# Scores of the differential heads: three fp32r products of split operands in place of one fp32 product, with a new tile order

## The chip, the cores and the metric

One core of a Trainium2 chip runs the whole kernel in one launch. The metric is the device time in microseconds of that launch, the median of several runs.

## What is computed

The kernel is one decoder layer over 512 positions of width 1024, in fp32. The normalised input `n` is projected by one wide matrix to the inputs of three branches: A, causal differential attention (8 heads, two softmax maps of 64 channels each per head, with a relative-position bias); B, a gated DeltaNet (8 heads, in chunks); C, cross-attention (4 heads) into 256 memory tokens. Each branch is projected, the three are merged by sigmoid gates, projected again and added to the input; a squared-ReLU MLP follows. The change touches branch A:

```python
s = jnp.einsum('bqhmd,bkhmd->bhmqk', qi, k, preferred_element_type=jnp.float32) * scale
s = s + bias;  s = jnp.where(dist >= 0, s, -jnp.inf)
p = jax.nn.softmax(s, axis=-1)
w = p[:, :, 0] - lam * p[:, :, 1]
o = jnp.einsum('bhqk,bkhe->bqhe', w.astype(v.dtype), v)
```

with 8 heads `h`, two maps `m`, 64 channels `d`, and 128 value channels `e`.

## The kernel before

**Main tiles.** All large products run on TensorE (PE) by weight tiles of 1024 x 128. A weight tile is loaded by DMA into `w_raw`, rounded by ScalarE (ACT, L1107) to the fp32r buffer `w_hi`, and VectorE (DVE, L1404) writes the rest to `w_lo`. In `weight_tile` PE then makes three fp32r products for each of 8 blocks of rows: high by high (L1903), low input by high weight (L1904), high input by low weight (L1905), each with 512 moving columns (256 for the 16 tiles of the memory, whose input is `m_hi`, `m_lo`). A tile's sum lies in one of two PSUM banks, `acc[:, t % 2]`; ACT copies it out ("evac", L1171 for the cross queries `cq`, L1175 for `aq`, `ak`, `av` of a head), and PE waits for that copy before it starts tile t + 2 (`acc_free`).

**Steps between the main tiles.** In the mixing part (up to about 790 us) the tiles are cut in quarters, and between the quarters PE makes the steps of the branches. Attention has, for every head h, the steps `av` (transposes of v, L2007), `as0` and `as1` (scores, L2012), `at` (transposes of the weights, L2018), `ap` (weights by v, L2023) and `ay` (transposes of the output, L2027); before them cross-attention has `cs` (scores, L1991), `ct` (L1997) and `cv` (L2002) for each of 4 heads. Each step waits for ACT and DVE to finish the step before it: DVE adds the bias (L1560) and takes the maxima (L1566), ACT takes the exponentials (L1231), DVE normalises and subtracts (L1584, L1588), and so on. The delta steps of branch B (L2046 to L2103, with many 32 x 32 products in L2062, L2066, L2068) run the same way for four pairs of heads.

**Scores.** `as0` makes the three largest score blocks that fit three PSUM banks, `as1` the other five. A block of map m and query block q has its 64 channels in rows 64m to 64m + 63 of PE's array, 128 queries as stationary columns and (q + 1) x 128 keys as moving columns. The operands lie in `qkv_T`, fp32, buffered for two heads:

```python
score_parts = {"as0": ((0, 3, 0), (1, 3, 512), (0, 1, 1280)),
               "as1": ((1, 2, 640), (0, 2, 128), (1, 1, 1280), (0, 0, 0), (1, 0, 512))}
```

(map, query block, first PSUM column).

**The order of the work.** `ORDER` (L89) gives the order of the main tiles by hand. `mixing_tiles` expands it and says in `need_free` which step must be over before a tile may be copied out: the tiles of heads 0 and 1 wait for the last `cv` (their place in SBUF held the cross-attention's data), those of head h for `as1` or `av` of head h - 2. `plan_order` then simulates the engines with the costs in `PE_US`, `ACT_US`, `DVE_US` and others, and gives each engine a fixed order of its work; PE takes a delta step before an attention step before a main quarter when each is ready by the plan. The plan is made when the kernel is built; on the chip every engine runs its own order and waits on semaphores.

**Memory.** The softmax weights lie in `p_a` (two maps), their transposes in `wT`, a buffer of its own. `hold` keeps 1280 columns free; after it `mv_T`, `cq_T` and `qkv_T` share one place at different times.

Of the kernel before, what the change touches and what calls it, by code (L numbers as in the profile page):

```python
# [29 lines left out]
P = 128  # L30
# [44 lines left out]
         "sb": 1.35, "cs": 3.44, "cv": 3.43, "as0": 1.3, "as1": 1.35, "at": 1.09, "ap": 2.24, "av": 0.44, "ay": 0.44}  # L75
# [132 lines left out]
def plan_order(tiles, need_free, n_first):  # L208
# [30 lines left out]
    old = lambda n: n >= n_first - 1  # L239

    for t in range(n_first, n_mix):
        for n, (a, b) in enumerate(parts[t]):
            add("PE", "main", ("main", t, a, b), (b - a) * (0.36 if short(t) else 0.681),
                [("DVE", "lo", t), ("ACT", "evac", t - 2)] if n == 0 else [])
# [72 lines left out]
    for i, (kind, h) in enumerate(attn):  # L317
# [26 lines left out]
    for r in range(2):  # L344
# [3 lines left out]
            "DVE": ("lo", "delta", "attn", "conv", "fin", "finz", "pre"), "POOL": ("delta", "gate", "pre"),  # L348
# [89 lines left out]
def build(nc, weights, x, mem, w_ba, params, consts, onehot, relb, post_g, y_dram, gate_dram, f_dram, frep_dram, out):  # L438
# [13 lines left out]
    n_z = {t: i for i, t in enumerate(z_tiles)}  # L452
    n_gate = {t: i for i, t in enumerate(gate_tiles)}
# [3 lines left out]
    with ExitStack() as ctx:  # L457
# [71 lines left out]
        def part_of(buf, n, width=QB):  # L529
# [38 lines left out]
        c3 = ExitStack()  # L568
        s3 = sb_in(c3)
        qkv_T = s3("qkv_T", [P, 2, 3, S])  # L570
        onehot_sb = strip[0:BUCKETS, 0:2, :].rearrange("p a b -> p (a b)")[:, 0:SPAN]
        c3.close()
# [87 lines left out]
        lam_exp = sem("lam_exp")  # L660
        a_mm = sem("a_mm")
# [58 lines left out]
        f_row = qkv_T[0:HA, 1, 2, 0:SPAN]  # L720
# [18 lines left out]
                       "as1": ((1, 2, 640), (0, 2, 128), (1, 1, 1280), (0, 0, 0), (1, 0, 512))}  # L739
        score_cols = {"as0": slice(0, 3), "as1": slice(3, 8)}  # L740
# [359 lines left out]
        def _(act):  # L1100
# [54 lines left out]
            def evacuate(t):  # L1155
# [16 lines left out]
                elif kind in ("aq", "ak", "av"):  # L1172
                    if (kind, j) == ("av", 1):
                        act.wait_ge(f_out, 16)
                    last = nc.scalar.copy(qkv_T[:, j % 2, ("aq", "ak", "av").index(kind)], bank)  # L1175
# [201 lines left out]
        def _(dve):  # L1377
# [192 lines left out]

            def attn_scale(i):
# [104 lines left out]
            def reload_hi(kk):  # L1676

                dve.wait_ge(y_pre[kk % 2], 16 * (kk // 2 + 1))
                if kk == 0:
# [5 lines left out]
                        "mem_norm": memory_norm, "mem_gain": memory_gain, "mem_lo": memory_lo}  # L1685
# [155 lines left out]
        def _(pe):  # L1841
# [99 lines left out]
            def main_part(t, k0, k1):  # L1941
# [32 lines left out]
            def attn(i):  # L1974
# [29 lines left out]
                elif kind == "av":  # L2004
                    pe.wait_ge(acc_free, TILES.index(("av", h)) + 1)
                    for s in range(ST):
                        last = nc.tensor.transpose(ps_a[:, 0, s * P:(s + 1) * P], qkv_T[:, h % 2, 2, s * P:(s + 1) * P], ident)  # L2007
# [379 lines left out]
```

## Time and profile before

| | us |
|---|---|
| median of 3 runs (lowest, highest) | 1335.35 (1334.2, 1338.17) |
| profiled execution, its own time | 1335.78 |
| its span from first to last instruction | 1334.0 |
| PE busy in the span | 1310.9 |
| DVE busy | 763.4 |
| ACT busy | 461.9 |

The profile shows one execution of the kernel. A matmul's time in it runs from its start to the end of its passage through the array, so that matmuls overlap; what one costs PE is the distance from its start to the start of the next. PE's weight loads have a line of their own (PEld). An fp32 product stands as two records, an fp32r product as one.

### The profile page before, as it was taken

The page shows a single profiled execution, that of the slowest core. Times are in us where ns is not written, and L with a number is a line of the kernel's source. Part 1 is how long each engine was busy: PE and PEld are TensorE (multiplying, and loading weights), DVE is VectorE, ACT ScalarE, POOL GpSimd, SP SyncE. Part 2 cuts the span into 40 slices and gives each one's busy share as a digit, 9 for nine tenths or more (in the row PEclk, how much of TensorE's full clock was granted, in tenths as well). Part 3 has the DMA queues.
Part 4 walks back from the last instruction along what each step waited for, and adds up shares of the span by engine and source line. Part 5 has one row for each costly group of instructions (what it writes and reads, how often), then busy time and mean ns, then how long its engine had stood idle before and what let it go on. Part 6 is the DMA issues. An engine that isn't in the chain of part 4 may idle for free.

```text
span 1334.0 us, 23822 instructions
## 1 busy us (share of the span) xinstructions
PE 1310.9 (98%) x10193; PEld 1094.6 (82%) x10193; DVE 763.4 (57%) x1305; ACT 461.9 (35%) x765; POOL 186.5 (14%) x128
## 2 busy tenths in 40 slices
PE   9999999999999999999999999999989999999997
PEld 8789988787788887888878888888788788888786
DVE  6885335576676577568955354555675522355335
ACT  5443433343353443443434222112432212222220
POOL 1023000013000023000321412233012200022000
PEclk9999999999999999999999999999999999999999
DMA  6155413222212322212222636644422333233311
GB/s 217 66 177 166 125 48 111 79 95 64 75 56 79 102 97 85 63 62 97 71 89 97 185 123 218 210 157 149 174 65 94 95 111 101 89 98 101 101 63 63
DMA packets 62832, 144.03 MB, mean 108 GB/s; under 512 B 5072, under 2 KB 28168, under 8 KB 62728
## 3 DMA queue, kind: packets, MB, share of 16 engines
q1 hardware_dynamic: 62728, 142.51, 33.1%
q8 instruction: 81, 1.33, 0.4%
q14 instruction: 23, 0.19, 0.0%
HBM read 127.79 MB, written 16.27 MB: 108 GB/s over the span
## 4 chain that ended last, share of the span: by engine, by line
PE 88%; DVE 7%; issue 3%; ACT 2%; DMA 1%; POOL 0%; SPq 0%; DVEq 0%; ACTq 0%; POOLq 0%
PE acc L1903 17%; PE acc L1905 16%; PE acc L1904 16%; PE ps_a L1904 2%; PE ps_a L1903 2%; PE ps_a L1905 2%; PE ps_a L2012 2%; PE ps_d L2090 2%; PE ps_a L2219 2%; PE ps_d L2219 2%; PE ps_a L2220 2%; PE ps_d L2220 2%; PE ps_d L2221 2%; PE ps_a L2221 2%; DVE w_lo L1404 1%
## 5 line engine op out<-in xcount | busy, mean ns | idle before, releaser
L1404 DVE TENSOR_TENSOR w_lo<-w_raw,w_hi 128x1024 fp32r<-128x1024 f32 x170 | 233.4, 1373 | 205.6 <-ACT w_hi L1107 205.0
L1107 ACT CAST w_hi<-w_raw 128x1024 fp32r<-128x1024 f32 x170 | 178.0, 1048 | 407.0 <-PE acc L1905 331.8
L1903 PE MATMUL acc<-n_hi,w_hi 128*128 128x512 f32 x744 | 303.2, 408 | 0.0
L1905 PE MATMUL acc<-n_hi,w_lo 128*128 128x512 f32 x744 | 290.7, 391 | 0.0
L1904 PE MATMUL acc<-n_lo,w_hi 128*128 128x512 f32 x744 | 290.2, 390 | 0.0
L1905 PEld LDWEIGHTS acc<-n_hi,w_lo 128*128 128x128 f32 x744 | 139.6, 188 | 30.2
L1903 PEld LDWEIGHTS acc<-n_hi,w_hi 128*128 128x128 f32 x744 | 139.9, 188 | 29.2 <-issue 2.2
L1904 PEld LDWEIGHTS acc<-n_lo,w_hi 128*128 128x128 f32 x744 | 140.1, 188 | 25.9 <-issue 0.7
L1095 POOL TENSOR_TENSOR h_lo<-sq,h_hi 128x512 fp32r<-128x512 f32 x32 | 41.4, 1293 | 276.4 <-DVE h_hi L1819 276.4
L1903 PE MATMUL acc<-y_hi,w_hi 128*128 128x512 f32 x192 | 74.8, 390 | 0.0
L1905 PE MATMUL acc<-y_hi,w_lo 128*128 128x512 f32 x192 | 74.7, 389 | 0.0
L1904 PE MATMUL acc<-y_lo,w_hi 128*128 128x512 f32 x192 | 74.7, 389 | 0.0
L1404 DVE TENSOR_TENSOR wx_lo<-w_raw,wx_hi 128x1024 fp32r<-128x1024 f32 x27 | 42.7, 1582 | 55.5 <-ACT wx_hi L1107 55.5
L1078 POOL TENSOR_SCALAR gate_st<-gate_st 128x512 f32<-128x512 f32 x24 | 25.3, 1056 | 310.0 <-ACT gate_st L1189 310.0
L1342 ACT ACTIVATE sq<-relu 128x512 f32<-128x512 f32 x32 | 20.2, 632 | 118.7 <-DVE relu L1817 118.7
L1520 DVE SCALAR_TENSOR_TENSOR conv_y<-conv_x,par,conv_y 128x512 f32<-128x512 f32 x72 | 57.2, 794 | 2.6
L1107 ACT CAST wx_hi<-w_raw 128x1024 fp32r<-128x1024 f32 x27 | 28.2, 1043 | 52.0 <-PE acc L2221 28.7
L1049 POOL TENSOR_TENSOR sums_hi<-cst,par 128x1024 fp32r<-128x1024 f32 x4 | 8.4, 2103 | 262.6 <-PE ps_d L2046 150.2
L1903 PEld LDWEIGHTS acc<-y_hi,w_hi 128*128 128x128 f32 x192 | 36.0, 188 | 7.7
L1905 PEld LDWEIGHTS acc<-y_hi,w_lo 128*128 128x128 f32 x192 | 36.0, 188 | 7.5
L1904 PEld LDWEIGHTS acc<-y_lo,w_hi 128*128 128x128 f32 x192 | 36.0, 188 | 7.3
L1231 ACT ACTIVATE p_a<-ps_a,smd 128x512 f32<-128x512 f32 (+3 forms) x64 | 32.9, 529 | 16.7 <-DVE smd L1568 16.7
(424 smaller groups left out, 2465.7 us busy)
## 6 DMA issues: line engine op xcount, KB each, us to landing
w_raw<-weights SPq DMA_DIRECT2D x200, 512.0 KB, 3.5
gate_scratch<-gate_st SPq DMA_DIRECT2D x24, 256.0 KB, 4.2
g_in<-gate_scratch SPq DMA_DIRECT2D x24, 256.0 KB, 3.9
y_raw<-y_scratch SPq DMA_DIRECT2D x16, 256.0 KB, 3.7
x_tok<-x SPq DMA_DIRECT2D x4, 512.0 KB, 5.2
y_scratch<-y_st SPq DMA_DIRECT2D x4, 512.0 KB, 2.7
y_scratch<-d_ET SPq DMA_DIRECT2D x4, 512.0 KB, 2.7
y_scratch<-y_st SPq DMA_DIRECT2D x8, 256.0 KB, 2.3
```

The lines of the kernel that those rows point to most:

```text
L1095: nc.gpsimd.tensor_tensor(h_lo[:, f % 16], sq[:, f % 2], h_hi[:, f % 16].bitcast(F32), ALU.subtract).then_inc(hl_ok, 1)
L1107: nc.scalar.copy(hi_of_tile(t), w_raw[:, t % RAW]).then_inc(hi_ready, 1)
L1231: last = nc.scalar.activation(p_a[:, m, pack_of[q]:pack_of[q] + w], flat(ps_a[:])[:, col:col + w], ACT.Exp, bias=nbs[:, n:n + 1], scale=SC ...
L1404: V_.tensor_tensor(lo_of_tile(t), w_raw[:, t % RAW], hi_of_tile(t).bitcast(F32), ALU.subtract).then_inc(lo_ready, 1)
L1520: ins = V_.scalar_tensor_tensor(out=y, in0=conv_x[:, n % 2, j:j + S], scalar=par[:, col + j:col + j + 1], in1=y, op0=ALU.mult, op1=ALU.add)
L1903: mm(bank, wh, hi_of(k), start=start and k == 0, stop=False)
L1904: mm(bank, wh, lo_of(k), start=False, stop=False)
L1905: last = mm(bank, wl, hi_of(k), start=False, stop=stop and k == KT - 1)
L2012: last = mm(ps[:, col:col + (q + 1) * P], qkv_T[rows_m, h % 2, 0, q * P:(q + 1) * P], qkv_T[rows_m, h % 2, 1, 0:(q + 1) * P], start=True, ...
L2219: mm(to, high, wh, start=kb == 0, stop=False)
L2220: mm(to, low, wh, start=False, stop=False)
L2221: return mm(to, high, wl, start=False, stop=kb == 2 * KT - 1)
```

## The change

1. `aq` and `ak` are copied out by ACT into an fp32r buffer `qk_hi`, and DVE writes the rest, `acc - qk_hi`, to `qk_lo` (a new step `scores_lo`, two for each head). `av` goes to `v_T`.
2. Each score block is the sum of three fp32r products: high by high, high queries by low keys, low queries by high keys. Blocks are taken in groups, and a block of one query block (128 keys) is made 256 columns wide, the rest being overwritten later.
3. PE waits in `as0` for the low part of the head's keys, and before main tile t + 2 for the low part of tile t if that is `aq` or `ak`. The planner has the same two waits, and a cost of 0.75 us for the DVE step.
4. `wT` is now `p_a[:, 1]`, `hold` is gone, and the places of the buffers of queries and keys change.
5. `ORDER` and the planner's costs of `as0` and `as1` change.

```diff
-"as0": 1.3, "as1": 1.35
+"as0": 1.05, "as1": 1.2
...
-ORDER = [("first", 0), ("z", 0), ("mem", 0), ("cq", 0), ("cq", 1), ("cq", 2), ("cq", 3), ("conv", 1), ("head", 0),
-         ("head", 1), ("gate", 1), ("conv", 2), ("head", 2), ("gate", 2), ("head", 3), ("z", 1), ("gate", 1),
-         ("head", 4), ("gate", 2), ("z", 2), ("head", 5), ("conv", 3), ("head", 6), ("gate", 2), ("head", 7),
-         ("gate", 13), ("z", 3)]
+ORDER = [("first", 0), ("z", 0), ("mem", 0), ("gate", 1), ("cq", 0), ("cq", 1), ("cq", 2), ("conv", 1), ("cq", 3),
+         ("head", 0), ("conv", 2), ("head", 1), ("head", 2), ("z", 1), ("gate", 1), ("head", 3), ("head", 4),
+         ("z", 2), ("conv", 3), ("gate", 5), ("head", 5), ("gate", 2), ("head", 6), ("gate", 3), ("head", 7),
+         ("gate", 3), ("z", 3), ("gate", 6)]
...
+            if kind in ("aq", "ak"):
+                add("DVE", "qk", ("qk", t), 0.75, [("ACT", "evac", t)])
...
+        if kind == "as0":
+            deps.append(("DVE", "qk", of[("ak", h)]))
...
-        wT = sa_("wT", [P, 10 * P])
+        wT = p_a[:, 1]
...
-        hold = sa_("hold", [P, 1280])
...
+        qk_hi = s3("qk_hi", [P, 2, 2, S], F32R)
+        qk_lo = s3("qk_lo", [P, 2, 2, S], F32R)
+        v_T = s3("v_T", [P, 2, S])
...
+        product_groups = {"as0": (((0, 3, 0), (1, 3, 512)), ((0, 1, 1280),)),
+                          "as1": (((0, 0, 0), (1, 0, 512)), ((0, 2, 128), (1, 2, 640)), ((1, 1, 1280),))}
...
+                dve.wait_ge(acc_free, t + 1)
+                V_.tensor_tensor(qk_lo[:, place[0], place[1]], acc[:, t % 2], qk_hi[:, place[0], place[1]].bitcast(F32),
+                                 ALU.subtract).then_inc(qkl_ready, 1)
...
+                    if TILES[t - 2][0] in ("aq", "ak"):
+                        pe.wait_ge(qkl_ready, qk_tiles.index(t - 2) + 1)
...
-                    for m, q, col in score_parts[kind]:
-                        rows_m = slice(DA * m, DA * m + DA)
-                        last = mm(ps[:, col:col + (q + 1) * P], qkv_T[rows_m, h % 2, 0, q * P:(q + 1) * P],
-                                  qkv_T[rows_m, h % 2, 1, 0:(q + 1) * P], start=True, stop=True)
+                    if kind == "as0":
+                        pe.wait_ge(qkl_ready, 2 * h + 2)
+                    for group in product_groups[kind]:
+                        for n, (left, right) in enumerate(((qk_hi, qk_hi), (qk_hi, qk_lo), (qk_lo, qk_hi))):
+                            for m, q, col in group:
+                                rows_m = slice(DA * m, DA * m + DA)
+                                width = max(q + 1, 2) * P
+                                last = mm(ps[:, col:col + width], left[rows_m, h % 2, 0, q * P:(q + 1) * P],
+                                          right[rows_m, h % 2, 1, 0:width], start=n == 0, stop=n == 2)
```

In `ORDER`, "first" stands for 9 tiles (6 of the convolution, 3 gates), "mem" for 16 tiles of 256 columns, "conv" for 6, "head" for 3 (`aq`, `ak`, `av`), "cq" and "z" for 2, and ("gate", n) for n tiles.

## Rows read from the trace of the kernel before

**Rows 1.** The page, part 1: busy time of each engine.

```profile
PE 1310.9 (98%) x10193; PEld 1094.6 (82%) x10193; DVE 763.4 (57%) x1305; ACT 461.9 (35%) x765; POOL 186.5 (14%) x128
```

**Rows 2.** Busy time by stretch: length, then PE, PEld, DVE, ACT, POOL.

```profile
0.00:133.40 133.40, 129.05 (x1242) 114.85 (x1243) 97.24 (x176) 60.48 (x92) 24.55 (x19) 1.00 0.47 157
133.40:300.00 166.60, 166.60 (x1339) 138.82 (x1337) 81.25 (x129) 65.36 (x114) 5.66 (x3) 1.00 0.28 92
300.00:360.00 60.00, 59.05 (x1081) 47.27 (x1080) 37.88 (x72) 22.48 (x46) 11.63 (x6) 1.00 0.24 73
360.00:500.00 140.00, 140.00 (x842) 116.12 (x841) 97.26 (x201) 61.88 (x122) 8.72 (x6) 1.00 0.26 82
500.00:667.00 167.00, 165.66 (x1825) 136.45 (x1825) 125.80 (x238) 70.57 (x139) 28.17 (x16) 1.00 0.24 75
667.00:770.00 103.00, 101.19 (x1353) 83.75 (x1351) 49.61 (x101) 36.24 (x66) 25.46 (x21) 1.00 0.42 127
```

**Rows 3.** Waits of the whole kernel: who, for whom, total, times, longest.

```profile
ACT w_hi L1107 <- PE acc L1905: 331.8, 105, 6.7
...
PE ps_a L2027 <- DVE o_a L1596: 1.3, 1, 1.3
PE ps_d L2066 <- DVE d_XB L1639: 1.1, 2, 0.7
```

**Rows 4.** PE groups by form: busy, mean ns of one; score products and a full-array fp32 form.

```profile
L2002 PE MATMUL ps_a<-pT_c,mv_tok 128*128 128x512 f32 x32 | 14.4, 592 | 0.0
...
L2012 PE MATMUL ps_a<-qkv_T 64*128 64x512 f32 x32 | 9.0, 641 | 0.0
```

**Rows 5.** Timeline around the first score step of a head.

```profile
516.44 0.39 PE L1905 MATMUL acc<-n_hi,w_lo 128*128 128x512 f32 x1
...
516.67 0.40 PE L1903 MATMUL acc<-n_hi,w_hi 128*128 128x512 f32 x1
...
516.91 0.39 PE L1904 MATMUL acc<-n_lo,w_hi 128*128 128x512 f32 x1
...
517.14 0.40 PE L1905 MATMUL acc<-n_hi,w_lo 128*128 128x512 f32 x1
...
517.46 1.55 PE L2012 MATMUL ps_a<-qkv_T 64*128 64x512 f32 x6
...
518.95 0.26 PE L2066 MATMUL ps_d<-d_TT,d_XB 32*32 32x32 f32 x8
```

**Rows 6.** The same step, weight loads only.

```profile
517.46 0.30 PEld L2012 LDWEIGHTS ps_a<-qkv_T 64*128 64x128 f32 x4 [0.36 <-issue]
518.00 0.19 PEld L2012 LDWEIGHTS ps_a<-qkv_T 64*128 64x128 f32 x1 [0.23 <-issue]
518.43 0.19 PEld L2012 LDWEIGHTS ps_a<-qkv_T 64*128 64x128 f32 x1 [0.24 <-issue]
```

**Rows 7.** Timeline around the second score step of the same head.

```profile
529.32 1.56 PE L2012 MATMUL ps_a<-qkv_T 64*128 64x384 f32 x10
530.81 0.50 PE L1903 MATMUL acc<-n_hi,w_hi 128*128 128x512 f32 x1
531.15 0.40 PE L1904 MATMUL acc<-n_lo,w_hi 128*128 128x512 f32 x1
531.39 0.40 PE L1905 MATMUL acc<-n_hi,w_lo 128*128 128x512 f32 x1
```

**Rows 8.** Timeline in the memory tiles, whose products have 256 columns.

```profile
96.53 0.28 PE L1904 MATMUL acc<-m_lo,w_hi 128*128 128x256 f32 x1
...
96.64 0.28 PE L1905 MATMUL acc<-m_hi,w_lo 128*128 128x256 f32 x1
...
96.76 0.28 PE L1903 MATMUL acc<-m_hi,w_hi 128*128 128x256 f32 x1
```

**Rows 9.** Chain of waits: start, us. The cross-attention of one head, with fp32 products.

```profile
226.14 3.45 PE ps_a L1991 x16
...
237.77 0.87 PE ps_a L1997 x8
...
241.38 3.43 PE ps_a L2002 x8
...
247.54 3.45 PE ps_a L1991 x16
...
259.18 0.87 PE ps_a L1997 x8
...
262.82 3.43 PE ps_a L2002 x8
```

**Rows 10.** DVE groups by form: the nearest to the added subtraction.

```profile
L1404 DVE TENSOR_TENSOR w_lo<-w_raw,w_hi 128x1024 fp32r<-128x1024 f32 x170 | 233.4, 1373 | 205.6 <-ACT w_hi L1107 205.0
...
L1771 DVE TENSOR_TENSOR g_tmp<-acc,g_in 128x512 f32<-128x512 f32 x16 | 11.1, 692 | 39.2 <-PE acc L1905 39.2
```

**Rows 11.** ACT group: copies of head tiles out of the accumulator.

```profile
L1175 ACT COPY qkv_T<-acc 128x512 f32<-128x512 f32 x24 | 14.0, 582 | 0.0
```

More of the change, by code:

```diff
@@ L74 @@
 PE_US = {"dE": 0.91, "dL": 1.79, "dA": 1.79, "dU": 1.79, "dW": 1.79, "T1": 0.55, "Za": 0.55, "Wb": 1.05, "Z5": 0.55, "W5": 0.9, "Zl": 1.2, "Wl": 1.2, "sa": 0.45,
-         "sb": 1.35, "cs": 3.44, "cv": 3.43, "as0": 1.3, "as1": 1.35, "at": 1.09, "ap": 2.24, "av": 0.44, "ay": 0.44}
+         "sb": 1.35, "cs": 3.44, "cv": 3.43, "as0": 1.05, "as1": 1.2, "at": 1.09, "ap": 2.24, "av": 0.44, "ay": 0.44}
 ACT_US = {"dk": 2.1, "dL": 1.6, "Wb": 0.45, "Z5": 0.45, "W5": 2.1, "Zl": 0.62, "sb": 0.45, "cs": 2.9, "as0": 2.3, "as1": 2.9, "at": 1.5, "ap": 0.65,
@@ L239, in plan_order @@
     old = lambda n: n >= n_first - 1
+    split_of = lambda t: [("DVE", "qk", t)] if tiles[t][0] in ("aq", "ak") else []
     for t in range(n_first, n_mix):
@@ L243, in plan_order @@
             add("PE", "main", ("main", t, a, b), (b - a) * (0.36 if short(t) else 0.681),
-                [("DVE", "lo", t), ("ACT", "evac", t - 2)] if n == 0 else [])
+                [("DVE", "lo", t), ("ACT", "evac", t - 2)] + split_of(t - 2) if n == 0 else [])
     for t in range(n_first + SPL - 1, n_mix + SPL):
@@ L347, in plan_order @@
     rank = {"PE": ("delta", "attn", "main"), "ACT": ("hi", "evac", "delta", "attn", "fin", "finz"),
-            "DVE": ("lo", "delta", "attn", "conv", "fin", "finz", "pre"), "POOL": ("delta", "gate", "pre"),
+            "DVE": ("lo", "qk", "delta", "attn", "conv", "fin", "finz", "pre"), "POOL": ("delta", "gate", "pre"),
             "SP": ("load", "gate", "y", "yb", "bias", "pre")}
@@ L452, in build @@
     n_z = {t: i for i, t in enumerate(z_tiles)}
+    qk_tiles = [t for t in range(N_MIX) if TILES[t][0] in ("aq", "ak")]
     n_gate = {t: i for i, t in enumerate(gate_tiles)}
@@ L553, in build @@
         p_a = sa_("p_a", [P, 2, 10 * P])
-        wT = sa_("wT", [P, 10 * P])
+        wT = p_a[:, 1]
         v_tok = sa_("v_tok", [P, S])
         o_a = sa_("o_a", [P, ST, P])
-        hold = sa_("hold", [P, 1280])
+        c3 = ExitStack()
+        s3 = sb_in(c3)
+        s3("before_qk", [P, 512])
+        qk_hi = s3("qk_hi", [P, 2, 2, S], F32R)
+        qk_lo = s3("qk_lo", [P, 2, 2, S], F32R)
+        v_T = s3("v_T", [P, 2, S])
+        c3.close()
+        sa_("before_cq", [P, 2560])
         c3 = ExitStack()
@@ L567, in build @@
         c3.close()
-        c3 = ExitStack()
-        s3 = sb_in(c3)
-        qkv_T = s3("qkv_T", [P, 2, 3, S])
         onehot_sb = strip[0:BUCKETS, 0:2, :].rearrange("p a b -> p (a b)")[:, 0:SPAN]
-        c3.close()
         c2.close()
@@ L660, in build @@
         lam_exp = sem("lam_exp")
+        qkl_ready = sem("qkl_ready")
         a_mm = sem("a_mm")
@@ L719, in build @@
         ealog = sml[:, 64:64 + HB]
-        f_row = qkv_T[0:HA, 1, 2, 0:SPAN]
+        f_row = v_T[0:HA, 1, 0:SPAN]
         p_a_scr = flat(conv_qk[:, 0, 0])
@@ L1171, in evacuate @@
                     last = nc.scalar.copy(cq_T[:, (j // 2) % 2, j % 2], bank)
-                elif kind in ("aq", "ak", "av"):
-                    if (kind, j) == ("av", 1):
+                elif kind in ("aq", "ak"):
+                    last = nc.scalar.copy(qk_hi[:, j % 2, ("aq", "ak").index(kind)], bank)
+                elif kind == "av":
+                    if j == 1:
                         act.wait_ge(f_out, 16)
-                    last = nc.scalar.copy(qkv_T[:, j % 2, ("aq", "ak", "av").index(kind)], bank)
+                    last = nc.scalar.copy(v_T[:, j % 2], bank)
                 elif kind in ("dq", "dk", "dv"):
@@ L1569, in attn, with scores_lo @@
                                      ALU.mult).then_inc(a_max, 1)
+            def scores_lo(t):
+                kind, h = TILES[t]
+                place = (h % 2, ("aq", "ak").index(kind))
+                dve.wait_ge(acc_free, t + 1)
+                V_.tensor_tensor(qk_lo[:, place[0], place[1]], acc[:, t % 2], qk_hi[:, place[0], place[1]].bitcast(F32),
+                                 ALU.subtract).then_inc(qkl_ready, 1)
             def attn_scale(i):
@@ L1684, in _ @@
                         "pre": reload_hi, "beta_in": beta_and_decay_inputs, "beta": beta_and_decay,
-                        "mem_norm": memory_norm, "mem_gain": memory_gain, "mem_lo": memory_lo}
+                        "qk": scores_lo, "mem_norm": memory_norm, "mem_gain": memory_gain, "mem_lo": memory_lo}
             for kind, *n in ORDER_OF["DVE"]:
@@ L2006, in attn @@
                     for s in range(ST):
-                        last = nc.tensor.transpose(ps_a[:, 0, s * P:(s + 1) * P], qkv_T[:, h % 2, 2, s * P:(s + 1) * P], ident)
+                        last = nc.tensor.transpose(ps_a[:, 0, s * P:(s + 1) * P], v_T[:, h % 2, s * P:(s + 1) * P], ident)
                 elif kind in ("as0", "as1"):
                     ps = flat(ps_a[:])
-                    for m, q, col in score_parts[kind]:
-                        rows_m = slice(DA * m, DA * m + DA)
-                        last = mm(ps[:, col:col + (q + 1) * P], qkv_T[rows_m, h % 2, 0, q * P:(q + 1) * P],
-                                  qkv_T[rows_m, h % 2, 1, 0:(q + 1) * P], start=True, stop=True)
+                    if kind == "as0":
[7 more added lines that the diff above has]
+                                          right[rows_m, h % 2, 1, 0:width], start=n == 0, stop=n == 2)
                 elif kind == "at":
```

## The prediction

> **What bounds the kernel now.** I read the page's busy shares first, then the busy time by stretch, then PE's own waits, then the places of the change. PE is busy for 1310.9 of 1334.0 us [rows 1]. Busy time of pipelined matmuls proves little alone, so the stretches matter: in the mixing part after 133.4 us PE has no idle time up to 300, and 0.95, 0, 1.34 and 1.81 us in the four stretches from 300 to 770 us, 4.1 us in all [rows 2]. The longest wait there is 1.3 us, in `ay`, for DVE [rows 3]. ACT in turn waits for PE for 331.8 us before it rounds the next weights [rows 3], so the supply of weights is behind PE's pace and not ahead of it. DVE is at 97.3 of 140 and 125.8 of 167 us in the dense stretches [rows 2]: high, with some room. So here the time is the sum of what PE issues. What PE saves is saved, if the fixed order of the work does not turn it into waiting.
>
> **Part 1, the score products.** A main product of 512 columns starts 0.23 us after the one before it [rows 5], one of 256 columns 0.11 to 0.12 us after [rows 8]; both are fp32r. An fp32 product is two records, each 0.43 us for 512 columns (8 in 3.43 us) and 0.215 us for 256 (16 in 3.45 us) [rows 9]. So one fp32 product costs 0.86 us where three fp32r ones cost 0.69: the change wins 0.17 us at 512 columns and about 0.07 at 256 (0.43 against 0.36), and loses at 128, which it makes 256 wide.
>
> The score blocks of the two maps lie in different halves of the array, and as fp32 they run two at a time: the 32 records of 512 columns last 641 ns each, 20.5 us one after the other, and cover 9.0 us [rows 4]; four weight loads pass in 0.30 us [rows 6]. Step `as0` should then cost 2 x 0.43 for the pair and 2 x 0.215 for the single block, 1.29 us. It takes 518.95 - 517.46 = 1.49 [rows 5]. The other 0.20 is at its ends: a first weight load that nothing hides, and the change to other work. I keep it. `as1` takes 530.81 - 529.32 = 1.49 as well [rows 7].
>
> After the change, if fp32r pairs run together too: `as0` is 3 x 0.23 (pair of 512) + 3 x 0.12 (single 256) + 0.20 = 1.25 us. `as1` is 3 x 0.12 (pair of 256) + 3 x 0.175 (pair of 384, midway between the two rows) + 3 x 0.12 + 0.20 = 1.44. The saving is 0.24 + 0.05 = 0.29 us a head, **2.3 us** for 8 heads, of 23.8 us that the sixteen steps take. Bounds of it: if weight loads of a pair come one after the other, nothing is left of it (pairs that don't overlap at all are a rival below); if the 0.20 at the ends goes too, 2.3 + 3.2 = 5.5 us.
>
> The trace has no fp32r pair on half the rows, so this term hangs on the pairing. The Trainium skill (TensorE: Matmul & The Clock Gate, Part 3, The mechanism) says that a weight load overlaps a matmul in flight only when the row group differs. By that rule each of the 15 steps of a head would bear a bare load. The main stream speaks against it: its loads all go to the same rows and its products are still 0.23 us apart [rows 5].
>
> **Part 2, DVE's subtraction.** 16 instructions of 128 x 512 from PSUM. The nearest rows are 0.69 us with a PSUM operand, and 1.37 us for twice the columns written as fp32r [rows 10]; I take 0.69, 11 us of DVE in 470 us. It lies beside PE. ACT's copies keep their number and their 0.58 us [rows 11].
>
> **Part 3, the new waits.** PE waits before tile t + 2 for the subtraction of tile t. Behind that wait stands everything on PE. The bank used to be free about 0.6 us after the tile's last product, and is now free after 0.6 + 0.7 + hops, some 1.5 us; PE needs it one tile later, 8 x 3 x 0.23 = 5.5 us. Cover: 4 us. It fails only if DVE comes more than 4 us late to the subtraction; what could hold it are items of up to 4.5 us by the plan, so a wait now and then of 1 us is possible, and I put 0 to 2 us for all 16, and 0.3 in the sum. The wait in `as0` is for `ak`, which is followed by the whole tile `av` and its transposes: nothing. On DVE the subtraction waits for ACT's copy, with the weight splits, on which PE's next tile hangs, queued behind it. These have run up to three tiles ahead: nothing.
>
> **Part 4, buffers.** `wT` in `p_a[:, 1]`: the second map is dead once the difference is formed, before `at` is copied out, and the squares that DVE puts there follow `ap`. The steps of attention are already serial. Nothing, and no bound but a planner's shift.
>
> **Part 5, the order.** The same tiles, 24 gates among them; the work of PE is equal. What can change is idle time and how many times PE changes between main tiles and steps. One change costs 0.32 - 0.23 = 0.09 us going in [rows 5] and 0.34 - 0.23 = 0.11 coming back [rows 7], 0.2 together. There are 62 attention and 116 delta steps; 10 more or fewer that stand alone are 2 us. The 4.1 us of idle time [rows 2] are the most that a better order can take away beside that. The new order lays five gates behind the last convolution and spreads seven of the thirteen that stood at the end; this should thin out DVE where it is dense. I take 1.3 us as gained (a third of the idle time), with ends of 6 gained and 6 lost.
>
> **Sum** against the profiled execution: 1335.8 - 2.3 + 0.3 - 1.3 = 1332.5. That execution lies 0.4 above the median, so I predict **1332.1 us**. Differences under 0.3%, 4 us, are about what a measurement of this kernel cannot tell from none; the forecast is inside it.
>
> **Rivals.**
> *The order gives more.* PE's idle time goes (4.1 us) and ten to fifteen lone steps join others (2 to 3 us): 1335.4 - 2.3 - 6.5 = 1326.6. For it: the idle time sits at single steps that came too early by under 1.5 us [rows 3], as a plan with wrong costs gives. Against it: the plan's costs of the other steps stay as they were. Chance of passing 4 us in all: 0.35.
>
> *The pairs run one after the other.* At fp32r each half of the array would deliver a column in half the time of an fp32 record. If PSUM or the array cannot take both streams, `as0` gets 3 x 0.23 and `as1` 3 x (0.12 + 0.175) more, 1.57 us a head, 12.6 in all: 1335.4 - 3.3 + 12.6 = 1344.7, slower. It decides from 18% of lost overlap (2.3 of 12.6) for the saving to be gone, and from 58% (7.3 of 12.6) for a slower kernel. Against it: the fp32 pairs show no loss, their step of 0.43 being that of the full array [rows 9], and the moving rows read are 64 + 64, as many as a main product reads. The fp32 records last somewhat longer in pairs (641 against 592 ns [rows 4]). Chance 0.07. The same page of the Trainium skill (Part 3, Measured speedup vs the span model) gives 3.07 for four row tiles; an estimate from it, with 77% of the ideal, is 30% on the pairs, 3.8 us, and a time of 1335.9. A loss of that size I give 0.07, counted as no change.
>
> *The cross-attention blocks head 0.* `cq` 3 now stands right before head 0, whose copies wait for the last `cv`. A cross head takes 18.7 us from `cs` to the end of `cv` [rows 9], so head 0's `av` tile can start about 0.6 + 0.5 + 18.7 + 1.7 = 21.5 us after `cq` 3. PE has two main tiles (11.0) and the three steps themselves (7.75), 18.8; one or two delta steps of 1.8 us close the gap. If DVE, with six convolution tiles just behind it, makes the chain 10 us longer, PE stands for that time: 1335.4 - 2.0 + 8 = 1341. It decides from some 5 us of delay. Against it: cross heads have run 21.4 us apart [rows 9], and pair 1 of the delta work becomes ready there. Chance 0.08.
>
> *Something else takes the saving* (the subtraction late in dense stretches, more lone steps), and the time stays within 2 us of before: inside "no change", with my forecast.
>
> **How the numbers follow.** Forecast and its neighbours within 4 us: 0.43, partial overlap 0.07, so "same" 0.50. Better order: 0.35. Serial pairs and the blocked head: 0.15. The range of 1325.5 to 1341.0 takes in the better order with its ends and the blocked head, and leaves out the serial pairs.
>
> **What would show it.** Right: `as0` 1.25 us and `as1` 1.44 us from first product to the next work, 24 records a head; pairs of 512 columns 0.23 us apart; sixteen subtractions near 0.69 us; PE idle in 300 to 770 us not over 4 us; no wait of PE for `qk_lo` over 1 us. Wrong: `as0` near 1.9 us (serial pairs); a wait of PE of several us before the first `av` tile; PE's idle time in the mixing part changed by more than the scores save.

## The result and the profile after

The changed kernel takes 1338.56 us (12 runs, 1335.94 to 1340.49), the kernel before 1335.27 (12 runs, 1333.22 to 1338.17): a ratio of 1.0023, 95% interval 1.0015 to 1.0031. It is slower by 3.3 us, clear of noise, though inside the 0.3% that the prediction called no change. I had forecast 3.2 us faster. The profiled execution took 1337.14 us, 1.4 below the median of its kernel and 1.4 above the profiled one of before; what the profiles show is the smaller part of the difference. One sign of being right failed, by little: PE is idle for 4.2 us in 300 to 770 us, where I had set 4.

The scores first. The timeline of `as0` of one head in the changed kernel, with the columns of [rows 5]:

```profile
550.57 0.50 PE L2041 MATMUL ps_a<-qk_hi 64*128 64x512 f32 x2
550.91 0.40 PE L2041 MATMUL ps_a<-qk_lo,qk_hi 64*128 64x512 f32 x2
551.14 0.39 PE L2041 MATMUL ps_a<-qk_hi,qk_lo 64*128 64x512 f32 x2
551.37 0.28 PE L2041 MATMUL ps_a<-qk_hi 64*128 64x256 f32 x1
551.49 0.28 PE L2041 MATMUL ps_a<-qk_lo,qk_hi 64*128 64x256 f32 x1
551.61 0.27 PE L2041 MATMUL ps_a<-qk_hi,qk_lo 64*128 64x256 f32 x1
551.81 0.50 PE L1925 MATMUL acc<-n_hi,w_hi 128*128 128x512 f32 x1
```

The pairs run together, 0.23 us from one pair to the next; the step takes 551.81 - 550.57 = 1.24 us where it took 1.49 [rows 5]. The 16 steps, `as0` and `as1`, take 21.4 us by the distances between starts, against 23.8. This part of the change does what was said.

Then the busy time by stretch of the changed kernel (length, then PE, PEld, DVE, ACT, POOL, as in [rows 2]), and below it three of PE's waits, as in [rows 3]:

```profile
133.40:300.00 166.60, 165.55 (x1590) 139.05 (x1588) 92.00 (x138) 65.78 (x116) 18.14 (x9) 1.00 0.27 87
300.00:360.00 60.00, 60.00 (x967) 47.89 (x954) 37.64 (x63) 25.72 (x52) 0.00 (x0) 1.00 0.23 72
360.00:500.00 140.00, 138.93 (x1223) 116.14 (x1221) 96.52 (x201) 54.74 (x102) 19.23 (x9) 1.00 0.25 80
500.00:667.00 167.00, 163.91 (x1734) 137.23 (x1720) 120.56 (x237) 70.44 (x137) 23.02 (x16) 1.00 0.26 83
667.00:770.00 103.00, 103.00 (x1037) 87.13 (x1025) 59.03 (x134) 41.49 (x84) 6.74 (x8) 1.00 0.30 93
770.00:933.80 163.80, 162.01 (x718) 133.34 (x717) 79.93 (x104) 35.98 (x37) 52.91 (x36) 1.00 0.59 186
```

```profile
PE ps_a L2047 <- DVE p_a L1610: 3.0, 1, 3.0
...
PE acc L1925 <- POOL y_lo L1084: 1.8, 2, 1.0
...
PE ps_a L2056 <- DVE o_a L1618: 0.9, 1, 0.9
```

From 133 to 934 us PE is idle for 1.05 + 0 + 1.07 + 3.09 + 0 + 1.79 = 7.0 us; before it was 4.1, all of it ahead of 770. The small old gaps are mostly gone. In their place `at` of head 5 (counted from 0) waits 3.0 us in one piece for VectorE (DVE), where the longest wait was 1.3 us, and the first products of the branches wait twice for `y_lo`, 1.8 us in all, which GpSimd (POOL) writes. So of the profiled 1.4 us, 2.9 are added idle time and -2.4 the scores; the other 0.9 is spread over the start (0.3) and changes too small to place.

**Why DVE was late.** The timeline of DVE and, in the second fence, of POOL in the changed kernel, around that wait:

```profile
635.17 7.41 DVE L1606 TENSOR_SCALAR p_a<-p_a,smd 128x128 f32<-128x128 f32 x4
642.62 1.94 DVE L1610 SCALAR_TENSOR_TENSOR p_a<-p_a,smd 128x128 f32<-128x128 f32 x4
```

```profile
635.10 2.38 POOL L1069 TENSOR_TENSOR d_SCR<-d_XB,cst 128x1024 f32<-128x1024 f32 x1 [3.10 <-ACT d_XB L1274]
637.41 0.96 POOL L1072 MEMSET d_TF<- 128x1024 f32 x1
638.32 2.00 POOL L1074 TENSOR_TENSOR d_KB<-d_K,e_in 128x1024 f32<-128x1024 f32 x1
640.40 1.90 POOL L1076 TENSOR_TENSOR d_K<-d_K,k_fac 128x1024 f32<-128x1024 f32 x1
```

Four multiplications by a scalar for each row, which take 1.27 us together where POOL is quiet, took 7.41 us, until POOL's fourth instruction was over. In the kernel before, no head's multiplications were lengthened so (the longest of the 32 took 0.48 us). Weight splits were, which take 1.22 us in the median; one of them in that kernel, begun beside an instruction of POOL of 2.48 us:

```profile
514.10 3.40 DVE L1404 TENSOR_TENSOR w_lo<-w_raw,w_hi 128x1024 fp32r<-128x1024 f32 x1
```

PE did not wait for it. What is new in the changed kernel is not that the two engines hold one another up, but which instruction of DVE it hits.

**Why `y_lo` was late.** The last `ay` came at 754.6 us in place of 731.8. The data of the first branch are read back only then, since their place in SBUF is attention's; the last `y_lo` was ready at 794.3, with the first branch tile due at 787.4. Before, it was ready at 768.0, 20 us ahead of its tile. How far attention moved can be counted in `ORDER`: ahead of head 7 stood 8 gate tiles (beside the three of "first"), now 12, and all other tiles there are the same. A tile is 24 products, 5.5 us, so four tiles are 22 us, and the last `ay` came 22.8 us later.

### The profile page after: what moved, and what is told of

Same layout as the page of the kernel before. It is cut to its first block, busy times and chain, and to the rows that moved or that the text cites. A ratio compares the mean times of both kernels' runs of the same rounds, so it can differ in the third digit from the quotient of the medians.

```text
span 1335.4 us, 23967 instructions
## 1 busy us (share of the span) xinstructions
PE 1309.1 (98%) x10257; PEld 1097.8 (82%) x10257; DVE 771.6 (58%) x1321; ACT 462.4 (35%) x765; POOL 186.1 (14%) x128
## 4 chain that ended last, share of the span: by engine, by line
PE 88%; DVE 6%; issue 2%; DMA 2%; ACT 1%; POOL 1%; SPq 0%; DVEq 0%; ACTq 0%; POOLq 0%
PE acc L1925 16%; PE acc L1927 16%; PE acc L1926 16%; PE ps_a L1926 2%; PE ps_a L1925 2%; PE ps_a L1927 2%; PE ps_d L2119 2%; PE ps_d L2248 2%; PE ps_a L2248 2%; PE ps_d L2249 2%; PE ps_a L2250 2%; PE ps_a L2249 2%; PE ps_d L2250 2%; PE ps_a L2041 2%; PE ps_a L2052 1%
## 5 line engine op out<-in xcount | busy, mean ns | idle before, releaser
L1418 DVE TENSOR_TENSOR w_lo<-w_raw,w_hi 128x1024 fp32r<-128x1024 f32 x170 | 229.7, 1352 | 173.1 <-ACT w_hi L1119 172.0
L1090 POOL TENSOR_SCALAR gate_st<-gate_st 128x512 f32<-128x512 f32 x24 | 22.4, 931 | 477.3 <-ACT gate_st L1203 477.3
L1925 PE MATMUL acc<-m_hi,w_hi 128*128 128x256 f32 x128 | 37.5, 293 | 0.0
L1927 PE MATMUL acc<-m_hi,w_lo 128*128 128x256 f32 x128 | 36.1, 282 | 0.7 <-issue 0.7
```

The lines of the kernel that those rows point to most:

```text
L1418: V_.tensor_tensor(lo_of_tile(t), w_raw[:, t % RAW], hi_of_tile(t).bitcast(F32), ALU.subtract).then_inc(lo_ready, 1)
L1925: mm(bank, wh, hi_of(k), start=start and k == 0, stop=False)
L1927: last = mm(bank, wl, hi_of(k), start=False, stop=stop and k == KT - 1)
```

## The experiments

Theory A: the order costs (collision and late end), the scores save 2.3 us. Rival B: the split operands cost, by the subtraction and the longer hold of the bank. Rival C: the scatter between executions. "The kernel before" in each ratio was run on the same chip in the same session.

### The order alone

```diff
-ORDER = (that of before)
+ORDER = (that of after)
```

in the kernel before, nothing else.

> The kernel before with the new ORDER and nothing else: fp32 scores, no subtraction, old buffers. Theory A (the order is what costs, the scores save 2.3 us as their steps do in the trace): 3.3 + 2.3, so about 5.5 us above the kernel before (1341), with the long wait of PE for head 5's normalisation and the waits for y_lo ahead of the first branch tile again there. Rival B (the split operands cost: the subtraction, the bank held longer, the waits on it): the order alone is within 1.5 us of the kernel before. Rival C (the scatter between runs is the cost, whatever the order): within 2 us, with runs spread over 4 us.

1349.54 us (4 runs), ratio 1.0113 (1.0100 to 1.0126). Every theory was far off. PE's waits in its profile:

```profile
PE acc L1903 <- POOL y_lo L1072: 7.2, 5, 2.9
PE ps_d L2068 <- issue: 3.3, 2, 1.9
```

The new order without the planner's new costs and waits gives another plan: attention ends at 777.6 us, the last `y_lo` is ready at 806.1, and PE waits 7.2 us. That is not the whole of it:

```profile
791.00:800.00 9.00, 4.94 (x12) 2.52 (x12) 4.11 (x5) 0.83 (x2) 5.33 (x5) 0.81 0.45 139
800.00:812.00 12.00, 8.82 (x21) 5.94 (x21) 3.11 (x5) 1.05 (x1) 4.69 (x4) 0.57 0.75 232
```

The granted clock (third column from the right) fell behind the waits to a mean of 0.81 and 0.57, that is to the lower of its two levels (1.2 in place of 2.4 GHz) for a good part of 21 us. The clock is at 0.50 for 13.6 of them, which costs 6.8 us. The predicted collision of head 5 is not in this profile.

### The scores alone

```diff
-ORDER = (that of after)
+ORDER = (that of before)
```

in the changed kernel.

> The changed kernel with the old ORDER (split operands, three fp32r products, shared buffer, costs of the planner as changed). Theory A: 2.3 us under the kernel before, about 1333.0, PE idle in the mixing part about as in the kernel before. Rival B: at or above the kernel before (1335 to 1339). If both the order and the scores are innocent alone and cost together (the plan depends on both), neither this nor the order alone is slower.

1345.5 us (6 runs, 1341.71 to 1351.24), ratio 1.0087 (1.0067 to 1.0107). Theory A falls in the form in which I had it: the parts don't add. Each half costs 11 to 15 us and both together 3.3. The wait that I had put at 0.3 us is here, in PE's waits:

```profile
PE acc L1925 <- DVE qk_lo L1590: 6.4, 3, 2.3
```

The timeline of one of the three, PE, ACT and DVE:

```profile
327.86 1.25 PE L2047 MATMUL ps_a<-cst,p_a 128*128 128x128 f32 x10
...
328.11 1.05 ACT L1119 CAST w_hi<-w_raw 128x1024 fp32r<-128x1024 f32 x1 [3.61 <-PE acc L1927]
...
329.19 1.23 DVE L1418 TENSOR_TENSOR w_lo<-w_raw,w_hi 128x1024 fp32r<-128x1024 f32 x1 [1.19 <-ACT w_hi L1119]
...
330.33 0.68 DVE L1590 TENSOR_TENSOR qk_lo<-acc,qk_hi 128x512 fp32r<-128x512 f32 x1
...
331.16 0.47 PE L1925 MATMUL acc<-n_hi,w_hi 128*128 128x512 f32 x1 [2.05 <-DVE qk_lo L1590]
```

The subtraction stands in DVE's fixed order behind a weight split. The split waits for ACT's rounding, and that for the last product of PE's own tile, whose weights it overwrites (idle 3.61 us until PE). So the subtraction cannot come before PE has ended its tile, and PE's next tile waits for the subtraction: rounding, split and subtraction, 1.05 + 1.23 + 0.68, pass with PE idle but for one step. The profiled execution was the fastest of the six; the profile does not show what the slower ones, up to 1351 us, had beside these waits.

### GpSimd held back in the changed kernel

```diff
                 elif kind == "dL":
                     pool.wait_ge(d_act, dA[i + 1])
+                    if p == 3:
+                        pool.wait_ge(a_dve, aD[a_idx[("as1", 5)] + 1])
```

> The changed kernel, with GpSimd waiting in step dL of pair 3 until head 5's normalisation is over, so that the two don't run side by side. In the trace of the changed kernel the four multiplications of that head took 8.5 us instead of 1.5 beside four GpSimd instructions, and PE then waited 3.0 us. Theory A1 (they contend for a port): the four take about 1.5 us, PE's wait of 3 us goes, and the time falls by 2 to 3 us to about 1336. Rival (VectorE was slow there for another reason, or PE would wait for GpSimd instead): the multiplications stay long, or the time does not move by more than 1 us.

1335.9 us (11 runs), ratio 1.0005 (0.9996 to 1.0014): 0.0018 of the time, 2.4 us, under the changed kernel's ratio. DVE's row there:

```profile
635.41 1.27 DVE L1608 TENSOR_SCALAR p_a<-p_a,smd 128x128 f32<-128x128 f32 x4
```

The four take 1.27 us and PE's wait is gone. Theory A1 holds: beside GpSimd the multiplications are held up, and that costs about what PE waited (2.4 us in the times, 3.0 in the profile; the two intervals only just don't touch). GpSimd's work now falls beside a weight split of DVE. First DVE, then POOL:

```profile
639.09 3.24 DVE L1420 TENSOR_TENSOR w_lo<-w_raw,w_hi 128x1024 fp32r<-128x1024 f32 x1 [0.42 <-ACT w_hi L1121]
642.25 0.68 DVE L1592 TENSOR_TENSOR qk_lo<-acc,qk_hi 128x512 fp32r<-128x512 f32 x1
```

```profile
638.84 2.40 POOL L1071 TENSOR_TENSOR d_SCR<-d_XB,cst 128x1024 f32<-128x1024 f32 x1 [6.61 <-DVE p_a L1612]
642.10 1.99 POOL L1076 TENSOR_TENSOR d_KB<-d_K,e_in 128x1024 f32<-128x1024 f32 x1
```

The split takes 3.24 us, and PE does not wait for it. The subtraction, which reads one operand from PSUM, keeps its 0.68 us beside GpSimd.

### Products of one map after those of the other

```diff
-                        for n, (left, right) in enumerate(((qk_hi, qk_hi), (qk_hi, qk_lo), (qk_lo, qk_hi))):
-                            for m, q, col in group:
+                        for m, q, col in group:
+                            for n, (left, right) in enumerate(((qk_hi, qk_hi), (qk_hi, qk_lo), (qk_lo, qk_hi))):
```

> The changed kernel with the three products of one block issued one after the other and then those of the other map's block, so that neighbours use the same half of the array. If the pairing is worth what the prediction says: as0 gains 3 x 0.23, as1 3 x (0.12 + 0.175), 1.57 us a head, some 12.6 us in all, 1351; a little less because the last product of one map and the first of the other still overlap. If fp32r products of the two halves never really ran together, the time does not change.

1338.95 us (8 runs), ratio 1.0028 (1.0018 to 1.0038), as the changed kernel. By my expectation that would mean that pairs never ran together. The timeline says otherwise:

```profile
321.69 0.51 PE L2041 MATMUL ps_a<-qk_hi 64*128 64x512 f32 x2
322.03 0.40 PE L2041 MATMUL ps_a<-qk_lo,qk_hi 64*128 64x512 f32 x2
322.26 0.40 PE L2041 MATMUL ps_a<-qk_hi,qk_lo 64*128 64x512 f32 x2
```

The program now has three products of map 0 and then three of map 1, and they still start two by two. So they start out of the order of the program: the reading is that PE takes a product for the free half of the array ahead of older ones that wait for the other half. That nothing between the program and PE changed the order is not shown; the two of a pair start 10 ns apart here and 3 to 4 ns apart in the changed kernel. The experiment could not undo the pairing and says nothing on its worth.

### The old order with the subtraction ahead of the split

```diff
+    act, dve = order["ACT"], order["DVE"]
+    for item in [i for i in dve if i[0] == "qk"]:
+        k = dve.index(item)
+        while dve[k - 1][0] == "lo" and act.index(("evac", item[1])) < act.index(("hi", dve[k - 1][1])):
+            dve[k - 1], dve[k], k = dve[k], dve[k - 1], k - 1
```

in `plan_order`, with `ORDER` of before.

> The changed scores with the old ORDER, and the subtraction moved ahead of the weight split that stands just before it on VectorE wherever ScalarE copies the tile out before it rounds those weights. In the trace with the old ORDER, PE waited three times 2.2 us for the subtraction, which stood behind a split that itself waited for PE's own tile. Theory B1 (that place in VectorE's order is what costs): the three waits (6.4 us) go, and with them the fall of the clock at 614 us or some of it; the time is 1333 to 1337. Rival (VectorE is simply too full for 16 more instructions): PE waits elsewhere for as long, and the time stays at 1342 or above.

1342.66 us (6 runs, 1337.1 to 1343.8), ratio 1.0047 (1.0032 to 1.0062). The waits for `qk_lo` are gone from its profile, and with them 0.4% of the time; B1 holds for that part. But 0.47% remains, and the time lies in the rival's range and not in B1's. In this profile, of the fastest of the six, PE's idle time from 133 to 934 us is 4.9 us against 4.1 before, so in it the waits did not come back elsewhere, which the rival needs. PE waits in it at 606 to 609 us for DVE at two delta and attention steps:

```profile
606.77 0.63 PE L2061 MATMUL ps_a<-cst,o_a 128*128 128x128 f32 x4 [0.96 <-DVE o_a L1623]
608.94 1.20 PE L2127 MATMUL ps_d<-state,d_SCR 128*128 128x128 f32 x4 [1.54 <-DVE d_LT L1691]
...
611.20 0.63 PE L1932 MATMUL acc<-n_hi,w_lo 128*128 128x512 f32 x1
611.62 0.63 PE L1930 MATMUL acc<-n_hi,w_hi 128*128 128x512 f32 x1
```

Behind them main products start 0.42 us apart in place of 0.23: the clock is at its lower level, for 6.8 us. What held the slower executions up no profile here shows.

### Head 5 three gates earlier

```diff
-         ("z", 2), ("conv", 3), ("gate", 5), ("head", 5), ("gate", 2), ("head", 6), ("gate", 3), ("head", 7),
+         ("z", 2), ("conv", 3), ("gate", 2), ("head", 5), ("gate", 5), ("head", 6), ("gate", 3), ("head", 7),
```

> The changed kernel with head 5 after two gate tiles instead of five (the other three behind it). In the changed kernel attention ended 23 us later than before (754 against 732 us), the high and low parts of the first branch's data came until 794 us, and PE waited 2 us for them. Theory A2 (the late end of attention is what PE pays for there): attention ends some 10 us earlier, and the wait for y_lo is gone. The plan around heads 5 to 7 changes too, so the collision of head 5 with GpSimd may be gone or another may come: the whole time is between 1333 (both gone) and 1339. Rival (GpSimd or the loads are too slow there whenever attention ends): the wait for y_lo stays.

1338.88 us (10 runs), ratio 1.0025 (1.0016 to 1.0034). A miss: attention ended at 764.5 us, later and not earlier. The collision was gone, other waits came (1.7 us for `o_a`, 1.8 us in a step of small products, 1.1 us for `qk_lo`, `y_lo` again), and the time was the same. The count of tiles says why theory A2 had no chance here: head 5 stands three gates earlier, but the three stand behind it, and ahead of head 7, which ends attention, are 12 gates as in the changed kernel. What made it 10 us later still, the profile does not single out.

### Both mends

GpSimd held back, and the subtraction ahead of the split, in the changed kernel with its own order.

> The changed kernel with GpSimd's wait of the earlier run and the subtraction ahead of the weight splits. With the new ORDER PE never waited for the subtraction, so if theory B1 is right for the old ORDER only, this is equal to the run with GpSimd's wait alone (1335.9) within 1.5 us. If the subtraction costs in the new ORDER through VectorE's lateness, it is faster by 1 to 3 us.

1334.72 us (11 runs), ratio 0.9994 (0.9986 to 1.0003), against 1.0005 for the first mend alone. The second is worth 0.0011, 1.5 us, with intervals that overlap, although the profile of the changed kernel shows no wait for `qk_lo`. That it lies in DVE's lateness elsewhere is not shown.

### The read-back sooner

```diff
+    for k in range(1, len(order["SP"])):
+        if order["SP"][k][0] == "pre" and order["SP"][k - 1][0] == "gate":
+            order["SP"][k - 1], order["SP"][k] = order["SP"][k], order["SP"][k - 1]
...
+                dve.wait_ge(yh_ready, kk + 1)
+                V_.tensor_tensor(y_lo[0][:, kk], y_st[:, kk % 2], y_hi[0][:, kk].bitcast(F32),
+                                 ALU.subtract).then_inc(yl_ready, 1)
...
-            pool_work = {"gate": scale_gate, "delta": delta, "pre": lambda kk: y_lo_tile(0, kk)}
+            pool_work = {"gate": scale_gate, "delta": delta, "pre": lambda kk: None}
```

on top of both mends.

> The run with both mends, and the first branch's data read back sooner: its low part is made on VectorE right behind the high part instead of on GpSimd, where it stood behind gates that wait for PE's own tiles, and SyncE issues each read-back ahead of the gate store just before it. Theory A2 (the late reload is what PE pays for ahead of the first branch tile): PE's wait for y_lo (1.2 us in the profile of the run with both mends) is gone, and with it at times a fall of the clock: 1332 to 1334 in the median, under the kernel before by 0.1 to 0.3%. Rival (the loads themselves come too late because attention ends at 751 us): the wait stays and the time too, 1334.7.

1333.93 us (12 runs, 1330.2 to 1336.35), ratio 0.9985 (0.9975 to 0.9995). PE no longer waits for `y_lo`, although attention ended at 754.7 us, as late as in the changed kernel: the way of the data back was what PE waited for, not the end of attention alone. Against the run with both mends (0.9994) the gain lies inside the intervals. The profile has one new gap near 329 us, with the clock lower behind it (0.62, third column from the right). PE's wait there, and the busy time of the stretch behind it:

```profile
PE ps_d L2110 <- issue: 1.6, 1, 1.6
```

```profile
330.60:334.00 3.40, 3.40 (x11) 2.64 (x11) 3.29 (x6) 0.28 (x1) 0.00 (x0) 0.62 0.25 98
```

The same steps ran without the gap in other profiles. What differs is a load of instructions on DMA queue q8. DMA queues of the changed kernel in 325 to 327.5 us:

```profile
q8 instruction: 1, 0.02, 3.1%
```

and of this version in 327.5 to 331 us, with none in 325 to 327.5:

```profile
q8 instruction: 1, 0.02, 1.8%
```

The ten profiles with the new `ORDER` or one near it fall in two: in five the load begins between 325.2 and 326.1 us and there is no gap, in five (both profiles of this version among them) between 327.9 and 328.5 and PE stands for 1.6 to 2.1 us. That the load is what PE waits for is not shown, nor what makes it late.

### fp32 scores in the mended plan

```diff
-                    last = nc.scalar.copy(qk_hi[:, j % 2, ("aq", "ak").index(kind)], bank)
+                    last = nc.scalar.copy(qk_hi[:, j % 2, ("aq", "ak").index(kind)].bitcast(F32), bank)
...
+                    for m, q, col in score_parts[kind]:
+                        rows_m = slice(DA * m, DA * m + DA)
+                        last = mm(ps[:, col:col + (q + 1) * P], qk_hi[rows_m, h % 2, 0, q * P:(q + 1) * P].bitcast(F32),
+                                  qk_hi[rows_m, h % 2, 1, 0:(q + 1) * P].bitcast(F32), start=True, stop=True)
```

in place of the three products, in the version with both mends.

> The run with both mends, with the scores as one fp32 product again, in the blocks and order of the kernel before, while the plan, the buffers, ScalarE's copies (fp32 now) and VectorE's sixteen subtractions (whose result is no longer used) stay as they are. This prices the three fp32r products alone. By the prediction's term and by the steps in the trace (23.8 us against 21.5): 2.3 us slower than the run with both mends. Rival (what PE saves in these steps is given back in waits for VectorE and ScalarE, which the steps feed): less than 1 us of difference.

1339.59 us (5 runs), ratio 1.0031 (1.0019 to 1.0043), against 0.9994: 0.0037, 4.9 us, and by the ends of the intervals at least 2.1. So the rival (less than 1 us) is out, and the 2.3 us that the steps save are seen in the time or nearly so. `as0` takes 1.49 us again:

```profile
555.35 1.55 PE L2045 MATMUL ps_a<-qk_hi 64*128 64x512 f32 x6
556.84 0.50 PE L1932 MATMUL acc<-n_hi,w_hi 128*128 128x512 f32 x1
```

Its profile also has a gap of 2.1 us near 329 us and two stretches at the lower clock, which the profile with both mends has not; without gap and stretches it is 3.2 us longer (the table below). So part of the surplus is not the products'.

### The changed kernel and the mended one, once more

> The changed kernel unchanged, for another profile and more times. In four of the eight profiles with the new ORDER PE stood 1.6 to 2.3 us inside a step of small products near 329 us, where a load of instructions came after 327.5 us instead of before 326, and the clock fell behind it; the first profile of the changed kernel did not have it, and its execution was 1.4 us under its median. Theory C (this stall comes to some executions of every kernel with this order and makes the spread): the median is again 1338 to 1339, and a profile of a slower execution has the stall. Rival (the stall belongs to the other kernels only): it is absent, and an execution above 1338 has other low-clock stretches.

1338.3 us (11 runs, 1336.28 to 1342.11), ratio 1.0025 (1.0016 to 1.0034). The profiled execution was again a quick one (1336.3) and has no gap near 329, so theory C is neither shown nor refuted for this kernel. The result repeats. What the profile adds is the clock behind the collision:

```profile
644.34 1.34 PE L2047 MATMUL ps_a<-cst,p_a 128*128 128x128 f32 x10 [2.95 <-DVE p_a L1610]
```

```profile
641.00:644.20 3.20, 0.39 (x2) 0.00 (x0) 3.17 (x6) 0.00 (x0) 0.94 (x1) 1.00 0.00 0
645.40:648.80 3.40, 3.40 (x11) 2.73 (x9) 1.99 (x3) 1.74 (x3) 1.66 (x1) 0.50 0.50 152
```

After 3 us of idle time PE works at a granted clock of 0.50 for 3.4 us, its products 0.43 us apart. That stretch does half of its work: another 1.7 us lost. In the first profile of the same kernel the clock did not fall there, but at 998 us.

> The version with all three mends unchanged, for a second measurement against the kernel before: 0.9975 to 0.9995 of its time again if the gain is real, 1.000 or above if it was the chip or chance. A profile without the stall near 329 us would have a span of about 1329 us, with it 1334.

1334.53 us (11 runs), ratio 0.9993 (0.9984 to 1.0002). The two measurements of this version give 0.9985 and 0.9993, a mean of 0.9989, 1.5 us. It is the best version here, by little: the first interval excludes 1 and the second just doesn't. Its profile has the gap near 329 us and a span of 1332.7.

**The spans side by side.** The clock falls in the kernel before too. In every profile PE waits 2.4 us for DVE (`relu`) between 990 and 1008 us, in the MLP. The stretch of 996 to 1000 us behind it, in the kernel before and then in the run with both mends, granted clock in the third column from the right:

```profile
996.00:1000.00 4.00, 4.00 (x11) 3.12 (x11) 2.96 (x3) 1.40 (x3) 1.27 (x1) 0.57 0.38 131
```

```profile
996.00:1000.00 4.00, 4.00 (x19) 3.30 (x19) 2.07 (x5) 1.40 (x3) 1.29 (x1) 1.00 0.38 131
```

So each profile has its own number of such stretches, each of 3.4 us at 0.50 and so a loss of 1.7 us, and that hides what the plans differ by. Without them and without the gap near 329 us (every profile ends in 2.4 to 5.6 us at 0.50, longest in the last row; these are left in):

| profile | span | gap near 329 | low clock at | lost by it | span without both |
|---|---|---|---|---|---|
| before | 1334.0 | | 996 | 1.7 | 1332.3 |
| changed | 1335.4 | | 998 | 1.7 | 1333.7 |
| changed, again | 1334.5 | | 645 | 1.7 | 1332.8 |
| GpSimd held back | 1330.2 | | | | 1330.2 |
| both mends | 1329.3 | | | | 1329.3 |
| all three | 1334.0 | 1.6 | 331, 997 | 3.4 | 1329.0 |
| all three, again | 1332.7 | 2.1 | 332 | 1.7 | 1328.9 |
| both mends, fp32 scores | 1338.0 | 2.1 | 332, 1001 | 3.4 | 1332.5 |

The last column is an estimate from one execution of each. By it the plans with two and three mends are 3.0 to 3.4 us under the kernel before, of which the scores are 2.4. In the medians the version with all three mends is 1.5 us under it; that the rest goes into gaps and low clock, which its two profiles both have, fits but is not shown.

## Why the prediction was wrong

**Part 1, the scores: right.** `as0` 1.24 us (predicted 1.25), `as1` 1.42 to 1.45 (1.44), pairs of 512 columns 0.23 us apart, 2.4 us saved by the steps (2.3). The rival of pairs one after the other is refuted by the records. The weight loads cost nothing there: the last three products of `as0` all use rows 0 to 63, start 0.12 us apart, and the load for the second begins while the first, of 551.37 and 0.28 us, still runs. The weight load in the step shown at the start:

```profile
551.37 0.18 PEld L2041 LDWEIGHTS ps_a<-qk_lo,qk_hi 64*128 64x128 f32 x1
```

The Trainium skill (TensorE: Matmul & The Clock Gate, Part 3, The mechanism) says that a weight load overlaps a matmul in flight only when the row group differs; this trace does not agree. The figure of 3.07 for four row tiles on the same page of the Trainium skill (Part 3, Measured speedup vs the span model), by which pairs would have lost 3.8 us by my estimate, did not show either, though no run here has four tiles: the step of a pair is that of a full-array product.

**Part 2, the subtraction: right in size** (0.68 us in the mean for 16, predicted 0.69).

**Part 3, the waits: wrong in its reason, and right for the changed kernel by luck.** The failed step is "These have run up to three tiles ahead: nothing". The depth of the buffer is not slack in the queue: the split of the weights three tiles on waits for PE's own tile, and whatever stands behind it on DVE does too. With the old order it cost 6.4 us in three waits, over my bound of 2; with the new order none is seen in its two profiles (1.1 us with head 5 moved), and moving the subtraction gave 1.5 us, inside the intervals.

**Part 5, the order: the step that failed.** I took 1.3 us as gained, "a third of the idle time", with ends of 6. The new plan removed most of the old gaps, as I had it, and put in 3.0 us for the collision and 1.8 for the late read-back, 2.9 us more idle time in the sum. I had looked at DVE's room by its busy share and not at which DVE instructions would come to lie beside POOL's; and I had written that the change "spreads seven of the thirteen" last gates without counting where they go. Four of them go ahead of head 7 and three stand right behind it; by that count the four put off the end of attention by 22 us, and with it the read-back of the first branch. The trace of before had 20 us of slack there. With GpSimd held back, the data read back sooner and the subtraction moved, the kernel is at 1333.9 and 1334.5, where I had forecast 1332.1 for a plan without such waits. With the new order only the first of the three mends moved the time beyond the intervals.

**What neither part had: the clock.** I priced a wait at its length. Behind a wait of 1.5 to 3 us of PE the clock fell in some executions and not in others, and each stretch of 3.4 us at 0.50 cost 1.7 us more (twice that at 608 us, 6.8 us among the first branch tiles with the order alone). Such stretches stood at 332, 608, 614, 645 or near 1000 us in the various profiles, the last in the kernel before too. This goes with the wider spread of the changed kernel (1336.3 to 1342.1 in one session, against 1334.3 to 1337.6 for the kernel before). The 1.4 us between its profiled execution and its median fits one such stretch; no profile of a slow execution of this kernel was caught, so that is not shown.

**The rivals.** The blocked head 0 did not come: no wait ahead of the first `av` tile but 0.6 us in a cross-attention step near 297 us. "The order gives more" is refuted. The outcome was nearest to "something else takes the saving", which I had counted with my forecast.

**Open.** The share of the 3.3 us that belongs to the clock; why the load of instructions near 328 us comes late in some profiles, and if it is what PE waits for; what made the slower executions with the old order.

## What to carry to other kernels

When an order made by a planner changes, price the change by its plan and not by the edit: here each half of an edit cost 11 to 15 us alone and 3 together. Count the tiles ahead of the last step of each stage, before and after: here that gave 22 us with no run at all. For each engine with a fixed order, ask of every added item what stands in front of it and whether that waits, by however many steps, for the engine that will wait for the item. Look at what the end of a moved stage releases, and at which VectorE instructions will lie beside GpSimd's. Before two profiles are compared by their spans, take out the stretches at the lower clock.

## What the runs showed of the hardware

VectorE's multiplications of an SBUF tensor by a scalar for each row, 0.29 to 0.48 us each when GpSimd is quiet, took 3.27, 1.10, 2.05 and 2.12 us beside four GpSimd instructions in SBUF, and 1.27 us in all once GpSimd was held back. The Trainium skill (SBUF — State Buffer, SBUF: two separate sides) says that the two engines share a pair of ports as an exclusive lock, held for a whole instruction, which VectorE takes in its two-port modes, and with two inputs in SBUF against a GpSimd instruction that reads SBUF. The trace agrees: each of VectorE's four instructions ended 0.08 to 0.28 us after the end of one of GpSimd's, a weight split with two SBUF inputs took 3.24 us in place of 1.22, and a subtraction with one operand in PSUM kept its 0.68 us. That the multiplications run in a two-port mode no row shows.

Products for the two halves of PE's array started out of the order in which the program has them: three for rows 0 to 63 and then three for rows 64 to 127 started in pairs 0.010 us apart.

Half of PE's array per product costs nothing at fp32r when the other half has a product of its own: pairs of 64 rows by 512 columns started 0.23 us after one another, as single products of 128 rows do.
